# Expert rows gathered earlier: one-head selections first, scores after each query tile, eight seats from the start

## The chip, the cores and the metric

The kernel runs on one core of a Trainium2 chip. The metric is the device time of one execution in microseconds (us), the median of three runs. The engines are named as in the profile: PE (matrix products), DVE (vector work), ACT (activations and copies), POOL (elementwise work, and the issue of indirect transfers) and SP (the issue of plain transfers). A core has 16 DMA engines, which serve the queues of SP, ACT and POOL.

## The reference, cut to what matters

Two transformer blocks run over 256 tokens of width 1024. The change lies in the second half of the first block, a feed-forward layer that picks single-neuron experts by product keys:

```
def chunk(xc):                                   # 128 tokens
    q = (xc @ w_pq).reshape(P_CHUNK, P_HEADS, 2, P_DK // 2)
    s = jnp.einsum('thpd,hpkd->thpk', q, sub_keys)
    s_top, i_top = lax.top_k(s, P_TOPK)
    cand = s_top[..., 0, :, None] + s_top[..., 1, None, :]
    best, ci = lax.top_k(cand.reshape(P_CHUNK, P_HEADS, P_TOPK * P_TOPK), P_TOPK)
    ...
    expert = e1 * N_KEYS + e2
    gate = jax.nn.softmax(best.astype(jnp.float32), axis=-1).astype(xc.dtype)
    act = jax.nn.gelu(jnp.einsum('thkd,td->thk', u_tab[expert], xc), approximate=False)
    return jnp.einsum('thk,thkd->td', gate * act, v_tab[expert])
```

Each of the 256 tokens has 8 heads with 16 picks each. Each pick reads one row of `u` and one of `v`, 1024 floats each. The kernel keeps the two side by side in one table `uv`, so a pick is one row of 8 KB. Tokens lie on the 128 partitions in two tiles. One gather fetches one pick of all 128 tokens of a tile, 1 MB, so there are 2 x 8 x 16 = 256 gathers (`PICKED`), 268 MB together.

## The kernel before, in words

Every engine has one program, in a fixed order; waits on counters (semaphores) are all that ties the engines together. The work around the change, in order:

- **Query tiles.** PE makes eight tiles `pq0` to `pq7` of 512 columns, one head each (two key halves). `pq0` is a plain product. The fourteen halves of the others are split products: ACT rounds a block of the weights (`weight_round(c)`), POOL subtracts to get the rest (the loop over `SPLITS`, one step per c), and PE adds three products (L680 twice, then L685). `pq m` uses the blocks c = `AT_PQ` + 2m - 2 and + 2m - 1. I write "split +6" for the POOL step of c = `AT_PQ` + 6.
- **Scores.** After every second query tile, PE makes two score tiles (one for each token tile) of two heads. ACT copies query and score tiles out of PSUM (L1226 is the helper that records every activation).
- **Selection.** DVE takes `UNITS` one by one, in `select`. A unit is a token tile and two heads. It finds the 16 best of each key half (`top16`), the 16 best sums, and the rows' numbers, and then counts `index_ready` up. At some points in it, `keep_up` slips in dot products that are due (`dots_due`).
- **The picks.** For pick q: POOL issues the gather into seat q % 8 (`gather`, L1635). DVE makes the dot product of the u half with the token (`dot`, L1911). ACT makes a diagonal matrix from GELU of it times the gate (`weigh`). PE adds the v half, scaled by it, to the sum (`add_rows`, L853) and counts `v_done` up. Gather q waits for `v_done` of pick q - 8, whose seat it takes.
- **Seats.** The eight seats of 8 KB per partition lie one after the other in the arena from 16384. The last three overlap what the split products of the query tiles read (`h_hi`, `top_lo`, `top_hi2`). So five gathers are issued ahead of split +9, and the rest after `pq7`.
- **Weights.** SP fills three ring buffers in order (`load`), each when a counter `w_used` says that its last user is through. `keys` go between the first and the second block of `w_pq`. Near the end of the picks, five blocks of the next block's `w_in2` (2 MB each) are issued: two into the arena (`in2_early`), three into the ring. After the last pick, PE turns the sums over and the next block's products begin.

Of the kernel before, what the change touches and what calls it, by code (L numbers as in the profile page):

```python
# [24 lines left out]
ACT = mybir.ActivationFunctionType  # L25
# [26 lines left out]
UNITS = [(t, h, 2) for t in range(TT) for h in range(0, PH, 2)]  # L52
# [70 lines left out]
def dots_due(calls):  # L123


    return max(0, 3 * (calls - 4) // 2)
# [55 lines left out]

def tile_plan():
# [4 lines left out]
    def add(name, n, reader):  # L188
        first[name] = len(readers)
        readers.extend([reader] * n)  # L190
# [17 lines left out]
    for m in range(8):  # L208
        add(f"pq{m}", 1, "act")
        if m % 2:  # L210
            add(f"scores0_{m // 2}", 1, "act")
            add(f"scores1_{m // 2}", 1, "act")
        if m == 1:
            add("tokens0", 1, "dve")
# [28 lines left out]
def build(nc, w, out):  # L243
# [3 lines left out]
    with ExitStack() as ctx:  # L247
# [104 lines left out]
        keys = ar(12288, 16 * P)  # L352
# [7 lines left out]
        seats = [ar(16384 + 2 * D * i, 2 * D) for i in range(SEATS)]  # L360
# [145 lines left out]
        def _(sp):  # L506
# [24 lines left out]
            for i in range(4):  # L531
                load(STREAM["w_pq"] + i, w["w_pq"][i])
                if i == 0:
                    sp.wait_ge(conv_proj, 4)
                    sp.dma_start(keys, w["keys"]).then_inc(in_keys, 16)

            sp.wait_ge(dot_done, PICKED - 2)
            for i in range(2):
                sp.dma_start(in2_early[i], w["w_in2"][i]).then_inc(in2_loaded[i], 16)
            for i in range(9):  # L540
                load(STREAM["w_in2"] + i, w["w_in2"][2 + i])
# [46 lines left out]
        def _(pe):  # L588
# [269 lines left out]
            def scores(t, g, frees):  # L858

                ps = tile(TILE[f"scores{t}_{g}"])  # L860
                for j in range(4):
                    hp = 4 * g + j
                    last = group(ps[:, j * P:(j + 1) * P],
                                 [(qpT[:, hp, t * P:(t + 1) * P], keys[:, hp * P:(hp + 1) * P])], 0 if j else frees)
                last.then_inc(tile_ready, 1)

            for m in range(8):
                ps = tile(TILE[f"pq{m}"])
                for j in range(2):
                    frees = 1 if (2 * m + j) % 4 == 0 else 0  # L870
                    if m == 0:
                        last = plain(ps[:, j * T:(j + 1) * T], use(STREAM["w_pq"]), j, hT, None if j else h_part, 1, frees)
                    else:
                        c = AT_PQ + 2 * m - 2 + j
                        last = split(ps[:, j * T:(j + 1) * T], c, c + 1, h_hi, top_lo, frees,
                                     (h_split, K) if m + j == 1 else None)
                last.then_inc(tile_ready, 1)
                if m % 2:
                    if m == 1:
                        pe.wait_ge(in_keys, 16)  # L880
                    pe.wait_ge(tile_free["act"], readers[:TILE[f"pq{m}"] + 1].count("act"))
                    for t in range(TT):
                        scores(t, m // 2, 1 if m == 7 and t == 0 else 0)
                    if m == 1:
                        by_rows(0)
                if m >= 5:
                    for q in (2 * m - 10, 2 * m - 9):
                        add_rows(q)
            for q in range(6, PICKED - 1):
                if q == PICKED // TT - SEATS:  # L890
                    pe.wait_ge(gate_ready, len(UNITS))
                    by_rows(1)
                if q == PICKED // TT:
                    pe.wait_ge(dot_done, q)
                add_rows(q)
# [320 lines left out]
        def _(act):  # L1216
# [205 lines left out]
            for m in range(8):  # L1422
                if m:
                    for c in range(AT_PQ + 2 * m + 1, min(AT_PQ + 2 * m + 3, SPLITS)):
                        weight_round(c)
                ps = take(TILE[f"pq{m}"])
                fn(flat(qpT[:, 2 * m:2 * m + 2, :]), ps[:, :], ACT.Copy).then_inc(tile_free["act"], 1)
                if m % 2:
                    for t in range(TT):
                        ps = take(TILE[f"scores{t}_{m // 2}"])  # L1430
                        fn(sc[:, t, 2 * m - 2:2 * m + 2, :].rearrange("p a b -> p (a b)"), ps[:, :],
                           ACT.Copy).then_inc(tile_free["act"], 1)
                if m == 3:
                    gates_exp(0)
                if m >= 5:
                    for q in (2 * m - 10, 2 * m - 9):
                        weigh(q)
            for q in range(6, PICKED):
# [172 lines left out]
        def _(pool):  # L1611
# [26 lines left out]
            for c in range(SPLITS):  # L1638
                if c == AT_PQ + 9:
                    for q in range(5):  # L1640
                        gather(q)
# [17 lines left out]
            pool.wait_ge(tile_ready, TILE["pq7"] + 1)  # L1659
            for q in range(5, PICKED):  # L1660
                gather(q)
# [12 lines left out]
        def _(dve):  # L1674
# [239 lines left out]
            def select(u, between):  # L1914
# [4 lines left out]
                for i in range(2 * nh):  # L1919
                    hp = 2 * h0 + i  # L1920
                    if hp % 4 == 0:
                        score = TILE[f"scores{t}_{hp // 4}"]
                        dve.wait_ge(tile_free["act"], readers[:score + 1].count("act"))
# [560 lines left out]
```

## Time and profile before

| | |
|---|---|
| median of 3 runs | 1595.55 us (1595.25 to 1600.18) |
| the profiled execution's own time | 1595.38 us |
| its span | 1593.6 us |
| mean granted clock of PE | 0.979 |
| busy, share of the span | PE 88%, DVE 55%, ACT 36%, POOL 30% |
| gathers (queue q0) | 268.45 MB of 475.86 MB |

The span runs from the first to the last recorded instruction. Times below are microseconds from its start. Busy time alone tells little here, since the kernel is a row of stages with different limits. The stage of the change lies between about 380 and 1090.

### The profile page before, as it was taken

To read this page: it belongs to the slowest core of one execution; us is meant where nothing else is said; L and a number is where in the kernel's file an instruction comes from. 1 tells how busy PE (TensorE), PEld (TensorE's weight loads), DVE (VectorE), ACT (ScalarE), POOL (GpSimd) and SP (SyncE) were. 2 spreads that over 40 slices of the span, in tenths; PEclk is the share of its full clock that TensorE was granted. 3 is DMA by queue.
4 is the path that set the end of the run, shared out by engine and by line. 5 is a ranking of instruction groups with operands and counts; after the bars stand their busy time and mean duration, and the time that the engine had idled before them with its cause. 6 is when DMAs were issued, how large, how long until landed. Compare 5 with 4: busy or idle time off the path is not lost.

```text
span 1593.6 us, 17624 instructions
## 1 busy us (share of the span) xinstructions
PE 1402.7 (88%) x6500; PEld 845.1 (53%) x6500; DVE 871.5 (55%) x2048; ACT 578.8 (36%) x1078; POOL 478.4 (30%) x379
## 2 busy tenths in 40 slices
PE   6999999998878777878777777779999999899997
PEld 3888766697743232322222222226778987455544
DVE  2699675554659999844444444444437532412113
ACT  2244364433433433433333333335485411212112
POOL 0556400165533333333333333330435500000000
PEclk9999999999999999999999999999999999999999
DMA  9457521052379999999999999997133247799994
GB/s 384 189 233 292 211 93 67 25 214 103 135 299 422 421 421 421 421 421 422 421 421 422 422 421 421 421 411 298 53 141 124 107 167 310 280 427 428 428 427 199
DMA packets 53076, 475.86 MB, mean 299 GB/s; under 512 B 6144, under 2 KB 6784, under 8 KB 7552
## 3 DMA queue, kind: packets, MB, share of 16 engines
q0 software_dynamic: 36864, 268.45, 40.6%
q1 hardware_dynamic: 14832, 203.46, 31.8%
q10 hardware_dynamic: 1296, 2.84, 0.5%
q8 instruction: 51, 0.84, 0.2%
q14 instruction: 33, 0.27, 0.0%
HBM read 473.68 MB, written 1.05 MB: 298 GB/s over the span
## 4 chain that ended last, share of the span: by engine, by line
PE 52%; DMA 32%; DVE 10%; ACT 4%; issue 2%; POOL 1%; SPq 0%; DVEq 0%; ACTq 0%; POOLq 0%
DMA arena<-in_uv,pick 26%; PE psD L607 15%; PE psD L680 8%; PE psD L1103 6%; PE psY L853 5%; PE psD L685 4%; DVE arena L1911 4%; PE psD L1112 3%; ACT arena L1226 2%; DMA arena<-in_experts 2%; DMA ring<-in_w_mod 2%; PE psY L788 2%; DMA ring<-in_w_in 2%; PE psD L803 1%; PE psY L773 1%
## 5 line engine op out<-in xcount | busy, mean ns | idle before, releaser
L853 PE MATMUL psY<-arena 128*128 128x512 f32 x1024 | 513.4, 632 | 135.8 <-ACT arena L1226 133.9
L853 PEld LDWEIGHTS psY<-arena 128*128 128x128 f32 x1024 | 183.1, 196 | 462.6 <-ACT arena L1226 310.1
L1635 POOL DMA_INDIRECT arena<-in_uv,pick x256 | 240.7, 940 | 397.6 <-PE psY L853 372.8
L1226 ACT ACTIVATE arena<-cst,pick 128x128 f32<-128x128 f32 x256 | 102.9, 402 | 396.8 <-DVE pick L1911 393.8
L1911 DVE CUSTOM_DVE_ANT_0 arena<-arena,psD 128x1024 f32<-128x1024 f32 x128 | 156.3, 1221 | 162.5 <-DMA arena<-in_uv,pick 162.5
L1911 DVE CUSTOM_DVE_ANT_0 arena<-arena,psY 128x1024 f32<-128x1024 f32 x128 | 154.7, 1216 | 86.2 <-DMA arena<-in_uv,pick 85.6
L1226 ACT ACTIVATE arena<-psD 64x512 f32<-64x512 f32 (+4 forms) x128 | 68.3, 538 | 286.4 <-PE psD L1103 105.5
L1226 ACT ACTIVATE arena<-arena 128x128 f32<-128x128 f32 (+3 forms) x299 | 129.7, 434 | 17.1 <-DVE arena L2260 3.8
L1656 POOL TENSOR_TENSOR ring_r<-ring,work_r 128x1024 fp32r<-128x1024 f32 x19 | 46.5, 2460 | 159.1 <-ACT work_r L1226 159.0
L607 PE MATMUL psD<-arena 128*128 128x256 f32 (+4 forms) x352 | 90.3, 399 | 4.0 <-ACT arena L1226 2.4
L1752 DVE SCALAR_TENSOR_TENSOR psY<-arena,pick,psY 128x256 f32<-128x256 f32 x224 | 89.2, 482 | 0.0
L607 PE MATMUL psD<-arena,ring 128*128 128x256 f32 (+1 forms) x304 | 74.2, 402 | 4.0 <-issue 3.5
L1226 ACT ACT_TABLE_LOAD x56 | 71.8, 1283 | 7.4 <-DVE pick L1911 4.8
L607 PEld LDWEIGHTS psD<-arena 128*128 128x128 f32 (+2 forms) x352 | 60.1, 190 | 16.4 <-issue 3.5
L607 PEld LDWEIGHTS psD<-arena,ring 128*128 128x128 f32 x304 | 58.7, 195 | 15.8 <-issue 7.0
L2332 DVE TENSOR_TENSOR yrow_lo<-psD,yrow_hi 64x512 fp32r<-64x512 f32 x32 | 22.0, 689 | 71.4 <-ACT yrow_hi L1226 70.9
L685 PE MATMUL psD<-h_hi,ring_r 128*128 128x256 f32 x336 | 47.5, 284 | 1.0 <-POOL ring_r L1656 0.9
L1226 ACT ACTIVATE arena<-psY 128x512 f32<-128x512 f32 x47 | 27.9, 596 | 54.5 <-PE psY L773 35.9
L685 PEld LDWEIGHTS psD<-h_hi,ring_r 128*128 128x128 f32 x336 | 43.3, 192 | 1.8 <-POOL ring_r L1656 1.8
L1226 ACT ACTIVATE arena<-xh 128x512 f32<-128x512 f32 (+1 forms) x17 | 11.9, 705 | 76.1 <-DVE xh L2197 57.2
L2325 DVE SCALAR_TENSOR_TENSOR arena<-psD,arena 64x512 f32<-64x512 f32 x16 | 12.1, 756 | 48.0 <-ACT arena L1226 47.8
L1103 PE MATMUL psD<-arena,xh 128*64 128x512 f32 x160 | 36.5, 594 | 1.2 <-DMA arena<-in_experts 1.1
(381 smaller groups left out, 2390.2 us busy)
## 6 DMA issues: line engine op xcount, KB each, us to landing
arena<-in_experts SPq DMA_DIRECT2D x30, 2048.0 KB, 19.9
ring<-in_w_in SPq DMA_DIRECT2D x18, 2048.0 KB, 10.0
ring<-in_experts SPq DMA_DIRECT2D x18, 2048.0 KB, 18.2
ring<-in_w_mod SPq DMA_DIRECT2D x12, 2048.0 KB, 9.3
ring<-in_w_pq SPq DMA_DIRECT2D x4, 2048.0 KB, 7.9
ring<-in_w_out SPq DMA_DIRECT2D x3, 2048.0 KB, 8.1
ring<-in_w_pw SPq DMA_DIRECT2D x2, 2048.0 KB, 8.1
ring<-in_w_o SPq DMA_DIRECT2D x2, 2048.0 KB, 10.6
```

The source lines that it names most:

```text
L607: last = nc.tensor.matmul(dst, a, b, start=(i == 0), stop=(i == len(pairs) - 1))
L680: last = nc.tensor.matmul(ps, hi[:, k * P:(k + 1) * P], x[:, k, :], start=(k + i == 0), stop=False)
L685: last = nc.tensor.matmul(ps, lo[:, k * P:(k + 1) * P], x_hi[:, k, :], start=False, stop=(k == K - 1))
L788: last = nc.tensor.matmul(aux(m // 2 % 2)[:, (m % 2) * T:(m % 2 + 1) * T], wt[:, k * 512 + (m % 4) * P:k * 512 + (m % 4 + 1) * P], convz[: ...
L853: last = nc.tensor.matmul(y_of[t][:, h * 512:(h + 1) * 512], diag[:, q % DIAGS, :], seats[q % SEATS][:, D + h * 512:D + (h + 1) * 512], st ...
L1103: last = nc.tensor.matmul(psD[bank][lo:lo + 64, :], lhs, wt[:, col:col + 512], start=(k == 0), stop=(k == K - 1))
L1112: last = nc.tensor.matmul(psD[bank][lo:lo + 64, :], hidT[:, f, 64 * side:64 * (side + 1)], wd[:, f * D + 8 * lo:f * D + 8 * lo + 512], sta ...
L1226: return nc.scalar.activation(dst, src, f, **kw)
L1635: nc.gpsimd.indirect_dma_start(seats[q % SEATS], None, w["uv"], bass.IndirectOffsetOnAxis(index[:, q:q + 1], 0)).then_inc(gathered[q % SEA ...
L1656: nc.gpsimd.tensor_tensor(split_at(ring_r, c), split_at(ring, c), split_hi(c).bitcast(F32), ALU.subtract).then_inc(u_lo_ready, 1)
L1752: s[j % 2] = mark(stt(cpart if j == TAPS - 2 else acc, y[:, j:j + T], conv_w[:, m * TAPS + j:m * TAPS + j + 1], acc, ALU.mult, ALU.add))
L1911: nc.vector.tensor_tensor_reduce(u_row, u_row, rows_of[t], 1.0, 0.0, ALU.mult, ALU.add, dots[:, q:q + 1]).then_inc(dot_done, 1)
```

## The change

1. The first unit of two heads becomes two units of one head, so there are nine.
2. Score tiles hold one head for both token tiles, and follow each query tile (`pick_order`): `pq0`, tokens, scores 0, `pq1`, then `pq m`, scores m - 1, and scores 7 last.
3. The eight seats move: one to 10432, five stay at 16384, and two go into the ring buffer of the second `w_pq` block. `keys` move to 12480, into space that holds `merged` until `x_ready` reaches 8, so their load waits for that.
4. Gathers 0 to 5 are issued ahead of split +6, gathers 6 and 7 ahead of +8 (after `pq3`), 8 and 9 ahead of +10, 10 to 14 ahead of +12, and the rest after +13.
5. Sums 0 and 1 follow scores 3, sums 2 to 6 scores 4, 7 to 11 scores 5, and 12 to 17 scores 6 (`ADDS`).
6. `keep_up` counts from the first call, not the fourth.
7. SP issues the two early blocks of `w_in2` and two ring blocks when `v_done` is 249. Before, all five went when `dot_done` was 254. The fifth, whose buffer holds the last two seats, now waits for `v_done` 256.

```diff
-UNITS = [(t, h, 2) for t in range(TT) for h in range(0, PH, 2)]
+UNITS = [(0, 0, 1), (0, 1, 1)] + [(t, h, 2) for t in range(TT) for h in range(0, PH, 2) if t or h]
+ADDS = [0, 0, 0, 0, 2, 7, 12, 18]
...
-    return max(0, 3 * (calls - 4) // 2)
+    return max(0, 3 * (calls - 1) // 2)
...
+def pick_order():
...
+    order = [("pq", 0), ("tokens", 0), ("scores", 0), ("pq", 1)]
+    for m in range(2, PH):
+        order += [("pq", m), ("scores", m - 1)]
+    return order + [("scores", PH - 1)]
...
-        keys = ar(12288, 16 * P)
+        keys = ar(12480, 16 * P)
...
-        seats = [ar(16384 + 2 * D * i, 2 * D) for i in range(SEATS)]
+        pq1 = ring[(STREAM["w_pq"] + 1) % RING]
+        seats = ([ar(10432, 2 * D)] + [ar(16384 + 2 * D * i, 2 * D) for i in range(5)] +
+                 [pq1[:, 0:2 * D], pq1[:, 2 * D:4 * D]])
...
                 if i == 0:
-                    sp.wait_ge(conv_proj, 4)
+                    sp.wait_ge(x_ready, K)
                     sp.dma_start(keys, w["keys"]).then_inc(in_keys, 16)
 
-            sp.wait_ge(dot_done, PICKED - 2)
+            sp.wait_ge(v_done, PICKED - SEATS + 1)
             for i in range(2):
                 sp.dma_start(in2_early[i], w["w_in2"][i]).then_inc(in2_loaded[i], 16)
-            for i in range(9):
+            for i in (1, 2, 0, 3, 4, 5, 6, 7, 8):
+                if i == 0:
+                    sp.wait_ge(v_done, PICKED)
                 load(STREAM["w_in2"] + i, w["w_in2"][2 + i])
...
+            for kind, m in pick_order():
+                if kind == "pq":
+                    pq(m)
+                elif kind == "tokens":
+                    by_rows(m)
+                else:
+                    scores(m)
+                    if 2 <= m < PH - 1:
+                        for q in range(ADDS[m], ADDS[m + 1]):
+                            add_rows(q)
+            for q in range(ADDS[-1], PICKED - 1):
...
+                    if m == 1:
+                        gates_exp(0)
+                    if 2 <= m < PH - 1:
+                        for q in range(ADDS[m], ADDS[m + 1]):
+                            weigh(q)
...
             for c in range(SPLITS):
-                if c == AT_PQ + 9:
-                    for q in range(5):
+                if c == AT_PQ + 6:
+                    for q in range(6):
+                        gather(q)
+                if c == AT_PQ + 8:
+                    pool.wait_ge(tile_ready, TILE["pq3"] + 1)
+                    for q in range(6, SEATS):
+                        gather(q)
+                if c == AT_PQ + 10:
+                    for q in range(SEATS, SEATS + 2):
+                        gather(q)
+                if c == AT_PQ + 12:
+                    for q in range(SEATS + 2, SEATS + 7):
                         gather(q)
...
-            pool.wait_ge(tile_ready, TILE["pq7"] + 1)
-            for q in range(5, PICKED):
+            for q in range(SEATS + 7, PICKED):
                 gather(q)
```

POOL's program around the query tiles, before (`ring_r<-ring` is a split, `in_uv,pick` a gather):

```order
57 L1656 TENSOR_TENSOR ring_r<-ring,top_hi 128x1024 [waits u_hi_ready]
58 L1635 DMA arena<-in_uv,pick 128x2048 [waits index_ready]
59 L1635 DMA arena<-in_uv,pick 128x2048 x4
60 L1656 TENSOR_TENSOR ring_r<-ring,work_r 128x1024 [waits u_hi_ready] x2
61 L1656 TENSOR_TENSOR ring_r<-ring,top_hi 128x1024 [waits u_hi_ready]
62 L1656 TENSOR_TENSOR ring_r<-ring,work_r 128x1024 [waits u_hi_ready] x2
63 L1635 DMA arena<-in_uv,pick 128x2048 [waits tile_ready]
64 L1635 DMA arena<-in_uv,pick 128x2048 x2
65 L1635 DMA arena<-in_uv,pick 128x2048 [waits v_done] x24
```

The row ahead of the five gathers is split +8. The five splits behind them are +9 to +13. After the change, from split +5 on:

```order
55 L1681 TENSOR_TENSOR ring_r<-ring,top_hi 128x1024 [waits u_hi_ready]
56 L1650 DMA arena<-in_uv,pick 128x2048 [waits index_ready]
57 L1650 DMA arena<-in_uv,pick 128x2048 x5
58 L1681 TENSOR_TENSOR ring_r<-ring,work_r 128x1024 [waits u_hi_ready] x2
59 L1650 DMA ring<-in_uv,pick 128x2048 [waits tile_ready]
60 L1650 DMA ring<-in_uv,pick 128x2048
61 L1681 TENSOR_TENSOR ring_r<-ring,top_hi 128x1024 [waits u_hi_ready]
62 L1681 TENSOR_TENSOR ring_r<-ring,work_r 128x1024 [waits u_hi_ready]
63 L1650 DMA arena<-in_uv,pick 128x2048 [waits v_done] x2
64 L1681 TENSOR_TENSOR ring_r<-ring,work_r 128x1024 [waits u_hi_ready]
65 L1681 TENSOR_TENSOR ring_r<-ring,top_hi 128x1024 [waits u_hi_ready]
66 L1650 DMA arena<-in_uv,pick 128x2048 [waits v_done] x4
```

Fifteen gathers now stand among the splits, and seven of these wait for sums. SP's program at the end of the picks, before (`in_w_in` of L539 are the two early blocks, of L512 the ring's):

```order
30 L512 DMA ring<-in_w_pq 128x4096 [waits w_used] x3
31 L539 DMA arena<-in_w_in 128x4096 [waits dot_done]
32 L539 DMA arena<-in_w_in 128x4096
33 L512 DMA ring<-in_w_in 128x4096 [waits w_used] x9
34 L512 DMA ring<-in_w_bsb 128x4096 [waits w_used]
```

The same place after the change:

```order
30 L520 DMA ring<-in_w_pq 128x4096 [waits w_used] x3
31 L547 DMA arena<-in_w_in 128x4096 [waits v_done]
32 L547 DMA arena<-in_w_in 128x4096
33 L520 DMA ring<-in_w_in 128x4096 [waits w_used] x2
34 L520 DMA ring<-in_w_in 128x4096 [waits w_used,v_done]
35 L520 DMA ring<-in_w_in 128x4096 [waits w_used] x6
```

Four blocks now stand ahead of the wait for the last sum, and all four may be issued while gathers are still under way.

## Rows read from the trace of the kernel before

**Rows 1.** The page: GB/s in 40 slices; the gathers' queue.

```profile
GB/s 384 189 233 292 211 93 67 25 214 103 135 299 422 421 421 421 421 421 422 421 421 422 422 421 421 421 411 298 53 141 124 107 167 310 280 427 428 428 427 199
...
q0 software_dynamic: 36864, 268.45, 40.6%
```

**Rows 2.** Windows: busy us of PE, PEld, DVE, ACT, POOL; clock, DMA share, GB/s.

```profile
422.00:424.00 2.00, 0.42 (x1) 0.43 (x2) 1.93 (x10) 1.86 (x5) 0.79 (x1) 0.72 0.09 37
424.00:426.00 2.00, 2.00 (x3) 0.75 (x3) 1.93 (x4) 0.25 (x1) 0.00 (x0) 0.50 0.05 12
...
428.00:447.00 19.00, 17.49 (x108) 13.90 (x106) 0.00 (x0) 3.10 (x7) 2.40 (x1) 0.96 0.00 0
```

**Rows 3.** POOL in order of time: start, duration, what, idle before and its releaser.

```profile
400.80 2.40 POOL L1656 TENSOR_TENSOR ring_r<-ring,work_r 128x1024 fp32r<-128x1024 f32 x1 [0.48 <-ACT work_r L1226]
...
407.26 1.15 POOL L1635 DMA_INDIRECT arena<-in_uv,pick  x1 [1.22 <-DVE pick L1988]
...
412.45 0.94 POOL L1635 DMA_INDIRECT arena<-in_uv,pick  x1 [0.30 <-issue]
...
447.18 0.95 POOL L1635 DMA_INDIRECT arena<-in_uv,pick  x1 [11.21 <-PE psD L685]
...
495.22 0.94 POOL L1635 DMA_INDIRECT arena<-in_uv,pick  x1 [5.06 <-PE psY L853]
...
1065.95 0.94 POOL L1635 DMA_INDIRECT arena<-in_uv,pick  x1 [1.54 <-PE psY L853]
```

**Rows 4.** DVE in order of time: selection, the first late dot, the last dot.

```profile
390.67 0.30 DVE L1886 MAX8 arena<-arena 128x8 f32<-128x128 f32 x1 [13.63 <-ACT arena L1226]
...
406.78 0.19 DVE L1988 TENSOR_TENSOR pick<-psD,arena 128x32 uint32<-128x32 f32 x1
...
452.62 1.22 DVE L1911 CUSTOM_DVE_ANT_0 arena<-arena,psY 128x1024 f32<-128x1024 f32 x1 [25.85 <-DMA arena<-in_uv,pick]
...
1081.30 1.22 DVE L1911 CUSTOM_DVE_ANT_0 arena<-arena,psD 128x1024 f32<-128x1024 f32 x1 [1.24 <-DMA arena<-in_uv,pick]
```

**Rows 5.** PE in order of time: last of pq0, two score tiles, sums.

```profile
376.83 5.39 PE L812 MATMUL psD<-xh,ring 128*128 128x256 f32 x20 [0.19 <-DVE xh L1877]
...
418.63 2.05 PE L607 MATMUL psD<-arena 128*128 128x128 f32 x16 [0.86 <-ACT arena L1226]
423.57 6.73 PE L853 MATMUL psY<-arena 128*128 128x512 f32 x8 [2.90 <-ACT arena L1226]
...
437.45 3.70 PE L853 MATMUL psY<-arena 128*128 128x512 f32 x8 [1.41 <-ACT arena L1226]
```

**Rows 6.** The chain in order of time: one half of a query tile.

```profile
409.13 1.92 PE psD L680 x16
411.05 0.96 PE psD L685 x8
```

**Rows 7.** ACT in order of time: copy of a score tile, then a table load.

```profile
420.71 0.60 ACT L1226 ACTIVATE arena<-psD 128x512 f32<-128x512 f32 x1 [0.29 <-PE psD L607]
421.33 1.28 ACT L1226 ACT_TABLE_LOAD   x1
```

**Rows 8.** SP at the end of the picks, in order of time.

```profile
1077.61 0.80 SPq L539 DMA_DIRECT2D arena<-in_w_in  x2
```

**Rows 9.** PE at the end of the picks, in order of time.

```profile
1066.18 1.98 PE L853 MATMUL psY<-arena 128*128 128x512 f32 x4 [0.50 <-ACT arena L1226]
...
1083.73 1.88 PE L853 MATMUL psY<-arena 128*128 128x512 f32 x4
...
1088.22 8.42 PE L607 MATMUL psD<-arena 128*128 128x256 f32 x32 [0.74 <-DVE arena L2024]
```

**Rows 10.** DMA queues in 1096 to 1098: packets, MB, share of 16 engines.

```profile
q1 hardware_dynamic: 44, 0.69, 80.3%
q10 hardware_dynamic: 45, 0.16, 19.7%
```

**Rows 11.** The same in 1079 to 1080: the gathers' queue.

```profile
q0 software_dynamic: 3, 0.02, 5.8%
```

More of the change, by code:

```diff
@@ L207, in tile_plan @@
     add("out", 4, "dve")
[L208 to L214, printed above, removed]
+    for kind, n in pick_order():
+        add(f"{kind}{n}", 1, "dve" if kind == "tokens" else "act")
     add("tokens1", 1, "dve")
@@ L856, in add_rows, with pq @@
                 last.then_inc(v_done, 1)
[L858 to L867, printed above, removed]
+            def pq(m):
                 ps = tile(TILE[f"pq{m}"])
@@ L877, in _, with scores @@
                 last.then_inc(tile_ready, 1)
[L878 to L889, printed above, removed]
+            def scores(m):
+                if m == 0:
+                    pe.wait_ge(in_keys, 16)
+                pe.wait_ge(tile_free["act"], readers[:TILE[f"pq{m}"] + 1].count("act"))
+                ps = tile(TILE[f"scores{m}"])
+                for t in range(TT):
+                    for j in range(2):
+                        hp, at = 2 * m + j, (2 * t + j) * P
+                        last = group(ps[:, at:at + P], [(qpT[:, hp, t * P:(t + 1) * P], keys[:, hp * P:(hp + 1) * P])],
+                                     1 if m == PH - 1 and t + j == 0 else 0)
+                last.then_inc(tile_ready, 1)
+            for kind, m in pick_order():
[9 more added lines that the diff above has]
+            for q in range(ADDS[-1], PICKED - 1):
                 if q == PICKED // TT - SEATS:
@@ L1420, in weigh @@
                 fn(d, d, ACT.Copy, scale=gate[:, q:q + 1]).then_inc(diag_ready, 1)
[L1422 to L1438, printed above, removed]
+            for kind, m in pick_order():
+                if kind == "pq":
+                    if m:
+                        for c in range(AT_PQ + 2 * m + 1, min(AT_PQ + 2 * m + 3, SPLITS)):
+                            weight_round(c)
+                    ps = take(TILE[f"pq{m}"])
+                    fn(flat(qpT[:, 2 * m:2 * m + 2, :]), ps[:, :], ACT.Copy).then_inc(tile_free["act"], 1)
+                elif kind == "scores":
+                    ps = take(TILE[f"scores{m}"])
+                    fn(sc[:, :, 2 * m:2 * m + 2, :].rearrange("p t a b -> p t (a b)"),
+                       ps.rearrange("p (t n) -> p t n", t=TT), ACT.Copy).then_inc(tile_free["act"], 1)
+                    if m == 1:
[3 more added lines that the diff above has]
+                            weigh(q)
+            for q in range(ADDS[-1], PICKED):
                 weigh(q)
@@ L1920, in select @@
                     hp = 2 * h0 + i
-                    if hp % 4 == 0:
-                        score = TILE[f"scores{t}_{hp // 4}"]
-                        dve.wait_ge(tile_free["act"], readers[:score + 1].count("act"))
+                    if hp % 2 == 0:
+                        dve.wait_ge(tile_free["act"], readers[:TILE[f"scores{hp // 2}"] + 1].count("act"))
                     top16(sc[:, t, hp, :], sc2[:, i, :], sv[:, i, :], si[:, i, :])
```

## The prediction, made before the changed kernel ran

> **What bounds the kernel now.** I read the page first. From slice 13 on its GB/s row stands at 421 or 422 and hardly moves until the picks are over, and the gathers' queue carries 268.45 MB in 36864 packets, 144 for each gather [rows 1]. So in this stage the DMA engines set the time: one gather is 1.0486 MB, and 1.0486 / 421 gives **2.49 us**. DVE, ACT and PE follow it. The windows then show where DMA is not full. Five gathers run early, are through by 422, and DMA carries nothing from 428 to 447 [rows 2]. POOL's timeline says why: gather 4 goes out at 412.45, gather 5 at 447.18, released by the last query tile on PE [rows 3]. DVE meanwhile stands 25.85 us before dot 5 [rows 4]. Two things follow. First, whatever fills that hole, or starts gather 0 sooner, takes its length off the end of the picks, if DMA then stays full. Second, the last dot (1081.30) is followed at once by sums and the next block, with PE waiting for DVE and not for a load at 1088.22 [rows 4, 9]. What delays the last gather delays the whole kernel.
>
> **The start of the gathers.** pq0 ends at 376.83 + 5.39 = 382.2 [rows 5]. The tokens' transposes lie beside ACT's copy of pq0, so scores 0 can run from 383.0. Two score tiles take 2.05 [rows 5], one 1.0, its copy 0.6 [rows 7]: selection begins at 384.7, where it began at 390.67. The first unit took 406.97 - 390.67 = 16.3 us to its row numbers [rows 4]. With one head the searches halve and the small operations don't, so it lies between 8 and 16 us. I take 10, since the searches are most of it: 394.8. POOL must have done splits up to +5, one in 2.4 us [rows 3], and is free at about 395.3. Gather 0 goes out at **395.5**, not 407.26. The six take 1.15 + 5 x 1.25 = 7.4 us of POOL [rows 3], so split +6 ends at 405.3. PE reaches its use of it at 405.3 too, so that costs nothing; were the unit 3 us slower, PE would stand 3 us.
>
> `keys` now wait for `x_ready`, and the second `w_pq` block queues behind them on SP: 3 MB, 7.5 us at 421. The residual is complete before the norm and pq0 [rows 5] come, and `keys` and the block are wanted only behind these. I put this at nothing; if the cover were short, everything behind pq0 would be late by what is missing, and I see no more than 3 us of that.
>
> **The pace from there.** From idle DMA, gather 5 was issued at 447.18 and dotted at 452.62, so a gather lands 5.4 us after its issue, or 2.49 after the one before it. Gathers 8 and up need the sum eight picks before. Now PE sets that: half a query tile takes 1.92 + 0.96 = 2.88 [rows 6], a tile 5.8, a score tile 1.0, a sum 3.70 / 2 = 1.85 [rows 5]. My schedule, in the order of the new program:
> pq1 384.0 to 389.8; pq2, scores 1 to 396.6; pq3, scores 2 to 403.4; pq4, scores 3 to 410.2. Then PE stands 2.9 us for ACT's copy, a table load of 1.28 and two activations, as it did at 423.57 [rows 5, 7]. There the granted clock fell to 0.50 and two sums took 6.73 instead of 3.70 [rows 2, 5]. I expect the same here: sums 0 and 1 end at 416.5 and 419.8. pq5 and scores 4 to 426.6, 1.5 of waiting, sums 2 to 6 (with 0.6 for the tables of the second unit's exponent) to 438.2. pq6 and scores 5 to 445.0, sums 7 to 11 from 446.6 to 455.9. pq7 and scores 6 to 462.7, sums 12 to 17 from 464.3 to 475.4, scores 7 to 476.4. Then ACT loads tables twice more, and sum 18 ends at 482.8.
>
> Landings by that: gathers 0 to 7 from 400.9 to 418.3 without a hole; 8 and 9 at 422.0 and 425.4; 10 (issued 430.1) at 435.5 and 14 at 445.5; 15 (448.6) at 454.0, 19 at 464.0; 20 (466.3) at 471.7, 25 at 484.1; 26 (482.8) at 488.2. So the holes are not gone but cut into five, 20 us together: with eight seats and sums at set places, PE recycles only 2, 5, 5 and 6 of them between query tiles. From gather 26 on seats come back at 1.85 each, faster than 2.49, and DMA stays full as it did before. In the kernel before gather 26 was issued later than its data needed (495.22, rows 3), with a backlog: it landed at 452.6 + 21 x 2.49 = 504.9. The gain is **504.9 - 488.2 = 16.7**. One DMA engine trails the others: the last landing is 1081.30, not 452.6 + 250 x 2.49 = 1075.1, and at 1079 the gathers' queue still moves three packets a microsecond [rows 11]. Holes let it catch up, so I add 1.8, a third of that lag: **-18.5**. Bounds: -10 if the sums come 7 us later than drawn, -38 if no hole remains (11.8 earlier start and 27 of hole).
>
> **The end of the gathers.** This is where I look for the price. Four blocks of `w_in2`, 8.4 MB, now go out when `v_done` is 249. Sum 248 ran at 1066.18 for 1.98 [rows 9], so in the old frame that is 1068.2, against 1077.61 before [rows 8], when only the last gather and a half was on the way. Counted from 1069, with the last landing at 1081.30, 12.3 us of gathers are left, 4.9 of them. How do two queues share? Where SP's and ACT's queues both had work, each moved as many packets as the other, 44 and 45, and the bytes went by packet size, 80.3% to 19.7% [rows 10]. A gather's row is 8 KB, a block's row 16 KB. One for one, gathers get a third of the bandwidth, and the last lands when all four blocks are through: 8.4 / 421 = 19.9 us late. The last gather before kept its 2.49 although blocks had begun [rows 11, 4], so what an engine already holds isn't pushed back; that is worth about one packet in nine: **+19**. Bounds: 0 if gathers go first; 20 if all four go between.
>
> The Trainium skill ("DMA: Bandwidth & Descriptors", "Queues, rings and completion order") says that an engine goes round the queues by whole packets of some 9 to 17 descriptors. By that a gather and a block would alternate, and four blocks would pass ahead of the last gather, 20 us. The rows above don't agree with so coarse a turn, since ACT's small transfer moved evenly beside SP's, yet the price is nearly the same.
>
> With a gather every 7.5 us PE stands long enough for the lower clock, and the last sum (1.88, rows 9) and the turns beside it slow down as the two sums at 423.57 did, 6.73 - 3.70 = **+3** (0 to 7). Nothing comes back for the blocks' earlier arrival, since PE did not wait for them at 1088.22 [rows 9]. The fifth block waits for the last sum, but is wanted only behind the products that start at 1088.22, and takes 5 us: nothing.
>
> **Other edits.** The number of query, score and add instructions stays. One more unit costs DVE some 3 us of small operations, hidden while it waits for gathers. Its second unit waits for ACT's exponent until about 430, behind scores 4; dots 7 to 11 are due by 446 and done by 442.
>
> **Sum.** 1595.4 - 18.5 + 19 + 3 = 1598.9; the profiled time of 1595.38 and the median of 1595.55 are the same for this purpose. I say 1598.5. What a measurement of this kernel tells from no change is about 0.3%, 4.8 us.
>
> **The rivals.**
> (a) What I expect, gain and loss nearly equal: 0.42, of which 0.36 within 0.3% and 0.06 above.
> (b) Gathers are not held up by blocks of another queue. For it: the last gather's even pace; against it: the equal packet counts [rows 10]. Then only the start counts, 1577 to 1580. 0.27.
> (c) The start gains more, because ACT or the clock let the sums come sooner and the holes shrink: each microsecond at sum 18 is one at the end. Holes of 10 instead of 20 give 1588.5. Nothing in the rows shortens PE's own 95 us from 382 on except the clock's 3. 0.13.
> (d) Slower: the DVE queue decides. Its second unit is behind an exponent that ACT does only after scores 4; if dots 7 to 11 are late, PE stands with pq6 done and pq7 behind the sums, and every later gather moves. From 5 us of it the end is slower than before by over 0.3%: 1604, at 8 us 1607. For it is that DVE has only 4 us to spare by my schedule; against it, that its dots are done in time by the same schedule. 0.18.
> That the change doesn't do what it says I give nothing: the order above shows it.
>
> **Range and chances.** The likeliest case alone gives 1593 to 1604. The range takes in (b) and most of (d): 1577 to 1605. Faster by over 0.3% is (b) and (c), 0.40; within 0.3% 0.36; slower is (d) and the top of (a), 0.24.
>
> **What would show it.** First gather at 395 (393 to 401); GB/s not zero between 428 and 447 but with holes near 427, 447 and 465; sums of 3.3 us for the first two; gather 26 issued near 483. At the end, the time from the issue of the first `w_in2` block to the last dot: 13 us if gathers go first, 32 if they share. It is this number on which the prediction stands or falls; the second is the issue of gather 26.

## The result and the profile after

The changed kernel takes **1601.24 us** (median of 8 runs, 1598.42 to 1604.7) where the kernel before takes 1595.4 beside it (8 runs, 1590.66 to 1600.18). The ratio is 1.0038, interval 1.0023 to 1.0053: 5.8 us slower. I had said 1598.5 and 1577 to 1605. The profiled execution has a span of 1596.4 us, against 1593.6 before.

The page of the changed kernel: GB/s in 40 slices, and the gathers' queue.

```profile
GB/s 392 198 221 309 186 106 53 54 106 222 310 324 392 421 421 421 420 421 421 422 421 422 421 422 421 421 401 86 53 135 130 107 161 316 272 428 428 427 427 203
...
q0 software_dynamic: 36864, 268.45, 40.8%
```

Beside [rows 1] the middle is the same 421. Slices 10 to 12 carry more (222, 310, 324 for 103, 135, 299), and slice 13 a little less. Bytes and packets of the gathers are the same. So the change acts at the two ends of the picks. First the start. POOL in order of time, first the one-head unit's gathers, then those that wait for a sum behind each query tile:

```profile
392.98 1.15 POOL L1650 DMA_INDIRECT arena<-in_uv,pick  x1 [0.17 <-issue]
...
405.28 0.96 POOL L1650 DMA_INDIRECT ring<-in_uv,pick  x1 [0.16 <-issue]
...
414.77 0.96 POOL L1650 DMA_INDIRECT arena<-in_uv,pick  x1 [2.60 <-PE psY L863]
...
427.67 0.96 POOL L1650 DMA_INDIRECT arena<-in_uv,pick  x1 [4.30 <-PE psY L863]
...
445.54 0.96 POOL L1650 DMA_INDIRECT ring<-in_uv,pick  x1 [4.30 <-PE psY L863]
...
462.44 0.94 POOL L1650 DMA_INDIRECT arena<-in_uv,pick  x1 [9.10 <-PE psY L863]
...
480.07 0.94 POOL L1650 DMA_INDIRECT arena<-in_uv,pick  x1 [8.11 <-PE psY L863]
```

These are gathers 0, 6, 8, 10, 15, 20 and 26. Gather 0 goes out 14.3 us sooner than in [rows 3] and gather 26 15.2 sooner. Part of that isn't the change's: pq0 ends at 374.19 + 5.32 = 379.5, 2.7 us sooner than in [rows 5]. Over the changed kernel and the variants of it that follow it ends anywhere from 379.5 to 383.8, though up to there they are all the same program. I count from the end of pq0 from here on. The windows (busy us of PE, PEld, DVE, ACT, POOL; clock, DMA share, GB/s) show four holes where [rows 2] has one. The last row is the whole stretch with them: 317 of 421 GB/s over 91 us is 22 us of DMA time not used.

```profile
422.00:428.00 6.00, 4.59 (x24) 3.06 (x23) 0.32 (x2) 5.39 (x10) 1.70 (x2) 1.00 0.07 26
...
443.00:446.00 3.00, 2.72 (x7) 1.29 (x8) 1.90 (x5) 2.87 (x9) 0.46 (x1) 1.00 0.16 68
...
460.00:463.00 3.00, 2.81 (x7) 1.38 (x8) 2.66 (x9) 2.81 (x9) 0.56 (x1) 1.00 0.13 55
...
480.00:482.00 2.00, 2.00 (x4) 0.80 (x3) 1.97 (x8) 1.53 (x4) 0.94 (x1) 0.62 0.45 98
...
483.00:600.00 117.00, 95.82 (x199) 37.19 (x197) 105.62 (x353) 45.80 (x103) 46.74 (x51) 0.96 1.01 419
...
399.00:490.00 91.00, 78.76 (x345) 50.15 (x344) 65.24 (x210) 39.14 (x78) 43.97 (x36) 0.92 0.82 317
```

Then the end. SP in order of time: the four `w_in2` blocks, two from each row.

```profile
1049.53 0.80 SPq L547 DMA_DIRECT2D arena<-in_w_in  x2
1050.38 0.91 SPq L520 DMA_DIRECT2D ring<-in_w_in  x2
```

DVE, the last five dots:

```profile
1052.74 1.22 DVE L1935 CUSTOM_DVE_ANT_0 arena<-arena,psD 128x1024 f32<-128x1024 f32 x1 [1.25 <-DMA arena<-in_uv,pick]
1058.91 1.22 DVE L1935 CUSTOM_DVE_ANT_0 arena<-arena,psD 128x1024 f32<-128x1024 f32 x1 [4.94 <-DMA arena<-in_uv,pick]
...
1066.28 1.22 DVE L1935 CUSTOM_DVE_ANT_0 arena<-arena,psD 128x1024 f32<-128x1024 f32 x1 [6.14 <-DMA arena<-in_uv,pick]
...
1073.67 1.22 DVE L1935 CUSTOM_DVE_ANT_0 ring<-ring,psD 128x1024 f32<-128x1024 f32 x1 [6.16 <-DMA ring<-in_uv,pick]
...
1081.00 1.22 DVE L1935 CUSTOM_DVE_ANT_0 ring<-ring,psD 128x1024 f32<-128x1024 f32 x1 [6.10 <-DMA ring<-in_uv,pick]
```

From the moment the blocks are out the dots come first 6.2 and then 7.4 us apart, not 2.5. The chain of the same stretch says what the end waits for, a gather that takes 33.70 us to land:

```profile
1047.28 33.70 DMA ring<-in_uv,pick
...
1081.00 1.22 DVE ring L1935
```

The two DMA queues in 1055 to 1060, then in 1070 to 1075 (packets, MB, share of 16 engines):

```profile
q1 hardware_dynamic: 104, 1.61, 75.5%
q0 software_dynamic: 76, 0.52, 24.7%
...
q1 hardware_dynamic: 130, 1.88, 88.6%
q0 software_dynamic: 7, 0.04, 2.0%
```

PE at the same end, against the 1.98, 1.88 and 8.42 of [rows 9]: a late sum at the lower clock, the last sum, and the next block.

```profile
1075.88 3.44 PE L863 MATMUL psY<-ring,arena 128*128 128x512 f32 x4 [3.67 <-ACT arena L1241]
...
1084.04 2.70 PE L863 MATMUL psY<-ring,arena 128*128 128x512 f32 x4
...
1089.36 8.42 PE L617 MATMUL psD<-arena 128*128 128x256 f32 x32 [0.73 <-DVE arena L2047]
```

### The profile page after: what moved, and what is told of

The parts are those of the page before. It is cut to its first block, busy times and chain, and to the rows that moved or that the text cites. A ratio compares the mean times of both kernels' runs of the same rounds, so it can differ in the third digit from the quotient of the medians.

```text
span 1596.4 us, 17667 instructions
## 1 busy us (share of the span) xinstructions
PE 1403.1 (88%) x6500; PEld 848.7 (53%) x6500; DVE 875.0 (55%) x2076; ACT 579.4 (36%) x1081; POOL 478.8 (30%) x379
## 4 chain that ended last, share of the span: by engine, by line
PE 54%; DMA 29%; DVE 9%; ACT 4%; issue 2%; POOL 1%; SPq 0%; DVEq 0%; ACTq 0%; POOLq 0%
DMA ring<-in_uv,pick 21%; PE psD L617 15%; PE psD L690 8%; PE psY L863 8%; PE psD L1118 6%; PE psD L695 4%; PE psD L1127 3%; DMA arena<-in_uv,pick 3%; ACT arena L1241 2%; DMA arena<-in_experts 2%; DVE ring L1935 2%; PE psY L798 2%; DMA ring<-in_w_in 2%; DVE arena L1935 1%; ACT L1241 1%
## 5 line engine op out<-in xcount | busy, mean ns | idle before, releaser
L863 PE MATMUL psY<-arena 128*128 128x512 f32 x768 | 389.9, 640 | 111.5 <-ACT arena L1241 111.2
L863 PEld LDWEIGHTS psY<-arena 128*128 128x128 f32 x768 | 139.8, 198 | 355.1 <-ACT arena L1241 237.4
L1650 POOL DMA_INDIRECT arena<-in_uv,pick x192 | 180.6, 940 | 309.0 <-PE psY L863 300.7
L1935 DVE CUSTOM_DVE_ANT_0 arena<-arena,psD 128x1024 f32<-128x1024 f32 x96 | 117.2, 1221 | 131.1 <-DMA arena<-in_uv,pick 131.1
L863 PE MATMUL psY<-ring,arena 128*128 128x512 f32 x256 | 126.7, 622 | 27.4 <-ACT arena L1241 27.3
L1935 DVE CUSTOM_DVE_ANT_0 arena<-arena,psY 128x1024 f32<-128x1024 f32 x96 | 115.9, 1215 | 41.6 <-DMA arena<-in_uv,pick 41.1
L1241 ACT ACTIVATE arena<-arena 128x128 f32<-128x128 f32 (+2 forms) x300 | 129.7, 433 | 17.1 <-DVE arena L2283 3.8
L863 PEld LDWEIGHTS psY<-ring,arena 128*128 128x128 f32 x256 | 45.9, 194 | 106.6 <-ACT arena L1241 67.9
L1650 POOL DMA_INDIRECT ring<-in_uv,pick x64 | 60.1, 940 | 86.7 <-PE psY L863 86.2
L1935 DVE CUSTOM_DVE_ANT_0 ring<-ring,psD 128x1024 f32<-128x1024 f32 x32 | 39.1, 1221 | 50.0 <-DMA ring<-in_uv,pick 50.0
```

The costliest lines, as they stand in the source:

```text
L863: last = nc.tensor.matmul(y_of[t][:, h * 512:(h + 1) * 512], diag[:, q % DIAGS, :], seats[q % SEATS][:, D + h * 512:D + (h + 1) * 512], st ...
L1241: return nc.scalar.activation(dst, src, f, **kw)
L1650: nc.gpsimd.indirect_dma_start(seats[q % SEATS], None, w["uv"], bass.IndirectOffsetOnAxis(index[:, q:q + 1], 0)).then_inc(gathered[q % SEA ...
L1935: nc.vector.tensor_tensor_reduce(u_row, u_row, rows_of[t], 1.0, 0.0, ALU.mult, ALU.add, dots[:, q:q + 1]).then_inc(dot_done, 1)
```

## The experiments

My theory: the start gains about 16 to 18 us, and the blocks beside the last gathers take it all back. The first rival: the start gains little and the blocks cost little. Nine kernels follow, each timed beside the kernel before, whose median was then 1595.4 to 1596.6. The table holds what the traces show, one profiled execution of each kernel, as distances, so that the spread of the stage ahead of pq0 drops out: from the end of pq0 to the start of gather 0, from there to the start of the last dot, from there to the next block's first product, and on to the end of the span.

```
kernel             median   ratio [interval]           pq0-g0  g0-dot  dot-block  block-end
before             1595.4   1                           25.0   674.0     6.9      505.4
changed            1601.2   1.0038 [1.0023, 1.0053]     13.5   688.0     8.4      507.0
late4              1578.9   0.9895 [0.9880, 0.9910]     13.5   669.6     6.9      507.8
before_early       1612.6   1.0103 [1.0088, 1.0119]     25.0   692.0     9.1      505.0
two_early          1590.7   0.9968 [0.9957, 0.9979]     13.5   682.0     6.8      504.9
quarter_pieces     1583.5   0.9920 [0.9904, 0.9937]     13.5   673.8     6.8      507.2
late4_after_dots   1583.9   0.9924 [0.9904, 0.9945]     13.5   669.5     9.1      507.7
late4_two_heads    1600.7   1.0031 [1.0018, 1.0044]     28.4   674.3     6.9      507.2
late4_keep         1578.1   0.9894 [0.9878, 0.9909]     13.5   666.5     6.9      506.8
late4_sums         1576.8   0.9884 [0.9869, 0.9899]     13.5   665.4     6.9      508.2
late4_sums_keep    1573.5   0.9857 [0.9838, 0.9876]     13.5   662.5     6.9      508.2
```

**late4.** The blocks wait for the dots again, everything else stays.

```diff
             sp.wait_ge(v_done, PICKED - SEATS + 1)
+            sp.wait_ge(dot_done, PICKED - 2)
```

> The changed kernel, with the four w_in2 blocks waiting for dot 254 as before, besides v_done 249. Theory 1 (the gain at the start was there, and blocks that share DMA with the last gathers took it back): the last gathers keep their 2.48 us, and the time is 20 to 25 us below the changed kernel, 1576 to 1581, and 15 to 19 below the kernel before. Rival (the gathers' DMA time is fixed and the new start brings little): within 4 us of the changed kernel, 1597 to 1605.

Measured 1578.85. SP, the last dot and the next block in its trace:

```profile
1059.10 0.80 SPq L548 DMA_DIRECT2D arena<-in_w_in  x2
```

```profile
1060.24 1.22 DVE L1936 CUSTOM_DVE_ANT_0 ring<-ring,psD 128x1024 f32<-128x1024 f32 x1 [1.23 <-DMA ring<-in_uv,pick]
...
1062.72 1.22 DVE L1936 CUSTOM_DVE_ANT_0 ring<-ring,psD 128x1024 f32<-128x1024 f32 x1 [1.24 <-DMA ring<-in_uv,pick]
```

The last gathers come 2.48 us apart to the end, and one line gives back 22.4 us by the medians. The two traces differ by 19.0 only; the profiled execution of the changed kernel was its fastest of eight, 1598.42 against the median of 1601.24. From pq0 to the last dot it is 683.1 us, against 699.1 before and 701.5 in the changed kernel: the start gains 16.0, the blocks cost 18.4.

**before_early.** The kernel before, with the changed kernel's early blocks alone.

```diff
-            sp.wait_ge(dot_done, PICKED - 2)
+            sp.wait_ge(v_done, PICKED - SEATS + 1)
```

> The kernel before, with one edit: the w_in2 blocks are issued at v_done 249 instead of dot 254. All five blocks go out here, since no seat lies in the ring. Theory 1: the last four gathers land 7.4 us apart instead of 2.48, and the time is 20 to 25 us above before, 1615 to 1621. Rival (the tail costs only together with the new seats, or not at all): 1593 to 1599.

Measured 1612.63, 17.2 us slower and 2.4 below the expected range. DVE's last dots:

```profile
1092.04 1.22 DVE L1911 CUSTOM_DVE_ANT_0 arena<-arena,psD 128x1024 f32<-128x1024 f32 x1 [6.15 <-DMA arena<-in_uv,pick]
...
1099.40 1.22 DVE L1911 CUSTOM_DVE_ANT_0 arena<-arena,psD 128x1024 f32<-128x1024 f32 x1 [6.13 <-DMA arena<-in_uv,pick]
```

The same 7.4 us, and the last dot 18.0 us later from gather 0. The cost is that of the blocks' moment, whatever the start does. It is also not that of their number: five blocks were out by 1070.14 here, and cost what four cost in the changed kernel. One block's worth passes ahead of each gather that is left, and there are four such gathers in both.

**two_early.** The changed kernel with two early blocks, the ring's two held until dot 254.

```diff
                 sp.dma_start(in2_early[i], w["w_in2"][i]).then_inc(in2_loaded[i], 16)
+            sp.wait_ge(dot_done, PICKED - 2)
```

> The changed kernel, with the two early blocks at v_done 249 and the two ring blocks at dot 254. If DMA packets alternate one for one, half the bytes cost half: two of the four late gathers are 7.4 us apart, and the time lies 10 to 11 us below the changed kernel, near 1590. If the loss came from the mere start of loads beside gathers, or from the lower PE clock, it would stay near 1600; if it came only from the ring blocks (whose buffers lie beside the last two seats), near 1579.

Measured 1590.65: 10.6 us of the 22.4 are back with half the bytes. The trace is less even. Up to the last dot only 6.0 of the 18.4 are back (682.0 beside 688.0 and 669.6). DVE's last dots:

```profile
1068.71 1.22 DVE L1936 CUSTOM_DVE_ANT_0 arena<-arena,psD 128x1024 f32<-128x1024 f32 x1 [6.12 <-DMA arena<-in_uv,pick]
...
1072.39 1.22 DVE L1936 CUSTOM_DVE_ANT_0 ring<-ring,psD 128x1024 f32<-128x1024 f32 x1 [2.45 <-DMA ring<-in_uv,pick]
...
1077.32 1.22 DVE L1936 CUSTOM_DVE_ANT_0 ring<-ring,psD 128x1024 f32<-128x1024 f32 x1 [3.70 <-DMA ring<-in_uv,pick]
```

Two gathers are 6.2 and 7.4 us apart, as expected; the last is 4.9, because the two ring blocks that went out at 1069.97 still met it.

**quarter_pieces.** The same four blocks at the same moment, in pieces of 4 KB a partition, with the waits on them raised to match.

```diff
-                sp.dma_start(in2_early[i], w["w_in2"][i]).then_inc(in2_loaded[i], 16)
+                for c in range(0, SLOT, 1024):
+                    sp.dma_start(in2_early[i][:, c:c + 1024], w["w_in2"][i][:, c:c + 1024]).then_inc(in2_loaded[i], 16)
...
-                sp.dma_start(ring[idx % RING][:, 0:n], src).then_inc(w_loaded[idx % RING], 16)
+                for c in (range(0, n, 1024) if idx in PIECES else (0,)):
+                    e = c + 1024 if idx in PIECES else n
+                    sp.dma_start(ring[idx % RING][:, c:e], src[:, c:e]).then_inc(w_loaded[idx % RING], 16)
```

> The changed kernel, with the four w_in2 blocks that start at the 249th sum each loaded as four loads of 4 KB a partition instead of one of 16 KB; same bytes, same moment, same queue. Theory (the engines take one packet of each queue in turn, whatever its size; the gathers' packets are 8 KB and the blocks' 16 KB, so the gathers get a third): with 4 KB packets the gathers get two thirds, the last ones come some 3.7 us apart instead of 7.4, the last dot is 8 to 12 us sooner after the first block's issue than the 31.5 us of the changed kernel, and the kernel takes 1588 to 1594 us. Rival 1 (the engines share by bytes, or the whole of one queue's ring entries goes first): the last gathers stay 7.4 us apart and the time within 2 us of the changed kernel's 1601. Rival 2 (sixteen starts on SP instead of four cost more than they give): slower than the changed kernel.

Measured 1583.54, 17.7 us faster than the changed kernel and 4 beyond the expected range. DVE's last dots, then the queues in 1061 to 1065:

```profile
1057.55 1.22 DVE L1943 CUSTOM_DVE_ANT_0 arena<-arena,psD 128x1024 f32<-128x1024 f32 x1 [2.22 <-DMA arena<-in_uv,pick]
...
1065.14 1.22 DVE L1943 CUSTOM_DVE_ANT_0 ring<-ring,psD 128x1024 f32<-128x1024 f32 x1 [2.54 <-DMA ring<-in_uv,pick]
...
1068.89 1.22 DVE L1943 CUSTOM_DVE_ANT_0 ring<-ring,psD 128x1024 f32<-128x1024 f32 x1 [2.53 <-DMA ring<-in_uv,pick]
```

```profile
q1 hardware_dynamic: 424, 1.54, 96.3%
q0 software_dynamic: 14, 0.10, 5.9%
```

Three gaps in 11.34 us are 3.78 each, as expected; I had only multiplied wrongly, for four gaps of 3.6 us less are 14.4, and the last dot came 14.2 sooner. The sum for one DMA engine: a gather is 1.0486 / 16 = 65.5 kB on it, eight rows of 8 KB, and takes 2.49 us alone. At that rate 7.37 us carry 194 kB, so 128 kB of a block pass per gather, eight packets of 16 KB; 3.78 us carry 99.5 kB, so 34 kB pass, eight packets of 4 KB. **Sharing goes by packets, not by bytes**: rival 1 of this run falls. Eight for eight would also come of turns of eight, and the changed kernel's last microseconds tell the two apart. By then the other engines are through with the gathers, and what sets the last dots is one engine that trails, as in [rows 11]. The queues in 1077 to 1078 of the changed kernel, then the gathers' queue in 1066 to 1067 of this run:

```profile
q1 hardware_dynamic: 3, 0.05, 11.5%
q0 software_dynamic: 1, 0.01, 1.9%
...
q0 software_dynamic: 3, 0.02, 5.8%
```

The second row, one gather packet in one microsecond, is the same in each of the four from 1076 to 1080. Turns of eight would show three of them a microsecond, as in [rows 11], and then none for 4.9 us. The shares give the times: 1.9% of 16 us is 0.31 for a gather's packet, 11.5% is 0.61 for each block packet. One of each takes 0.92 us, and eight pairs 7.4, the distance of the dots. With the small pieces two, three and two gather packets pass in the three microseconds from 1065. So the engine takes **one packet of each queue in turn**.

**late4_after_dots.** The blocks wait for dot 256 instead of 254.

```diff
-            sp.wait_ge(dot_done, PICKED - 2)
+            sp.wait_ge(dot_done, PICKED)
```

> late4 with the wait ahead of the w_in2 loads moved from the 254th dot to the 256th, so that no load shares the engines with a gather at all, and the loads go out about 5 us later. Theory 1 (the last gathers are held up only by what runs beside them, and in late4 nothing does any more): the dots are where they are in late4, and the loads come 5 us late for the next block, which costs 0 to 5 us: 1579 to 1584. Theory 2 (late4 still loses to the overlap at its end): a gain of 1 to 3 us against late4.

Measured 1583.9. The dots don't move (669.5 and 669.6), and PE now waits for the load at the next block:

```profile
1074.21 8.86 PE L618 MATMUL psD<-arena 128*128 128x256 f32 x32 [2.87 <-DMA arena<-in_w_in]
```

Theory 1: 254 costs the gathers nothing, and two dots later costs the next block 2 us in the trace and 5 by the medians. Of these two moments the old one is the better.

**late4_two_heads.** Every unit holds two heads again, and `keep_up` counts from the fourth call; score tiles, seats and the places of the gathers stay changed.

```diff
-UNITS = [(0, 0, 1), (0, 1, 1)] + [(t, h, 2) for t in range(TT) for h in range(0, PH, 2) if t or h]
+UNITS = [(t, h, 2) for t in range(TT) for h in range(0, PH, 2)]
...
-    return max(0, 3 * (calls - 1) // 2)
+    return max(0, 3 * (calls - 4) // 2)
```

> late4 with every top-k unit of two heads as before, so that gather 0 waits for the selection of two heads (12.5 us later by the changed kernel's own rows); everything else of the change stays. Theory (the one-head units carry most of what the change gives at the start): the row of gathers starts 12 us later and ends about 12 us later, 1589 to 1593 us, near the time of the kernel before. Rival (the start is paced by the sums between query tiles, not by when the first gather goes out): at most 4 us slower than late4, 1579 to 1583.

Measured 1600.67, 21.8 us above late4 and 8 beyond what I expected. I had reckoned 12.5 us for gather 0; the trace has 28.4 - 13.5 = 14.9, and then 4.7 more up to the last dot. DVE's selection shows the first part:

```profile
386.35 0.29 DVE L1911 MAX8 arena<-arena 128x8 f32<-128x128 f32 x1 [7.59 <-ACT arena L1242]
...
398.75 0.29 DVE L1911 MAX8 arena<-arena 128x8 f32<-128x128 f32 x1 [9.16 <-ACT arena L1242]
```

The second head's scores now come one query tile later, so a two-head unit stands 9.16 us for them. Cut scores without cut units are **worse** than the kernel before: gather 0 comes 3.4 us later from pq0 than there. Together the two edits bring gather 0 11.5 us sooner from pq0 (25.0 and 13.5), most of the 16.0 gained. One-head units with the old score tiles weren't run, and how much of the 4.7 is due to `keep_up` isn't shown.

**late4_keep.** Filler matmuls on PE between score tile 3 and sum 0, so that the clock doesn't fall while PE stands for ACT.

```diff
                     scores(m)
+                    if m == 3:
+                        keep(3, aux(2))
```

> As late4, and three idle 128x512 products on PE between scores 3 and sum 0, so that PE doesn't stand 2.9 us there. They write the half of PSUM that sum 0 begins anew. If the granted clock fell because PE stood, sums 0 and 1 take 3.7 us instead of 6.7, everything up to sum 18 is 3 us earlier, and the time is 2 to 3 us below late4. If the clock falls for another reason, the time is that of late4 or up to 1 us above it.

Measured 1578.08, 0.8 us below late4, where 2 to 3 were expected; that small a difference is within the error. The trace shows more. The filler takes 2.74 us, and sum 0 begins 31.2 us behind pq0 with it and without it, so it delays nothing. The granted clock at the sums is 1.00 instead of 0.50, and sums 0 and 1 take 3.70 instead of 6.67. Gather 26 goes out 3.0 us sooner from pq0, and the last dot comes 3.1 sooner from gather 0.

**late4_sums.** More sums at each stop between query tiles.

```diff
-ADDS = [0, 0, 0, 0, 2, 7, 12, 18]
+ADDS = [0, 0, 0, 0, 2, 8, 17, 28]
...
-                    for q in range(SEATS, SEATS + 2):
+                    for q in range(SEATS, SEATS + ADDS[4]):
...
-                    for q in range(SEATS + 2, SEATS + 7):
+                    for q in range(SEATS + ADDS[4], SEATS + ADDS[5]):
...
-            for q in range(SEATS + 7, PICKED):
+            for q in range(SEATS + ADDS[5], PICKED):
```

> late4 with the hand table of sums moved forward: sums 2 to 7 after score tile 4, 8 to 16 after score tile 5, 17 to 27 after score tile 6 (late4: 2 to 6, 7 to 11, 12 to 17), with the gathers ahead of the later splits moved to match. Theory (the start is paced by when sums free seats, which shows as three stretches of 3 us with q0 nearly empty in the changed kernel, near 425, 444 and 461): more sums per stop fill the last two of them, so gather 26 goes out some 5 us sooner than in late4 and the kernel takes about 1573 us (1571 to 1576). Rival 1 (the DVE, which does the dots between pieces of its selection, is the pace): the dots come no sooner, TensorE stands at the sums instead, and the time stays within 1.5 us of late4. Rival 2 (TensorE's query tiles are pushed back and the selection with them): slower than late4 by 2 to 5 us.

Measured 1576.78, 0.8 us above the expected range. In the trace gather 26 goes out 5.4 us sooner from pq0 than in late4, as expected, and the last dot comes 4.2 sooner from gather 0. The medians, from two different comparisons, give 2.1, so the size rests on one trace of each. Part of it is the clock: in late4 PE stands 4.38 us ahead of its first sums behind score tile 7 and does four of them in 9.86 us. First late4, then late4_sums, PE at that place:

```profile
476.19 9.86 PE L864 MATMUL psY<-arena 128*128 128x512 f32 x16 [4.38 <-ACT arena L1242]
```

```profile
476.75 7.13 PE L864 MATMUL psY<-arena 128*128 128x512 f32 x16 [1.71 <-ACT arena L1242]
```

**late4_sums_keep.** Both.

> late4 with both small additions, the sums moved forward in the hand table and the filler matmuls ahead of sum 0: if the two gains measured apart (1.7 and 0.8 us by the medians, each near what its measurement can tell) add up, 1576 us (1574.5 to 1578), the fastest of all. If the filler only delays sum 0 as it shortens it, and the sums' table already covers that, it is 1576 to 1578, as with the table alone.

Measured **1573.46**, the fastest, and 1 us below the expected range: 23 us under the kernel before and 28 under the changed one. From gather 0 to the last dot it is 7.1 us less than late4, 3.1 and 4.2 added; the medians give 5.4, 3.3 of it from late4_sums to here, for the filler.

## Why the prediction was right, and where it wasn't

- **What bounds the kernel**: right. DMA at 421, both ends of the picks decide, and the chain's 33.70 us gather says so again.
- **First gather at 395.5**: pq0-g0 was 13.5 us against 13.3 by my working. The one-head unit's row numbers were there at 391.99, 9.95 us behind its start at 382.04, where I took 10. As in my working it was split +5 that held the gather, here for the last 0.8 us. No engine stood for `keys`. DVE, then POOL:

```profile
391.82 0.17 DVE L2011 TENSOR_TENSOR pick<-psD,arena 128x16 uint32<-128x16 f32 x1
...
390.41 2.40 POOL L1681 TENSOR_TENSOR ring_r<-ring,top_hi 128x1024 fp32r<-128x1024 f32 x1 [0.46 <-ACT top_hi L1241]
```

- **The schedule by hand**: gather 26 was to go out 482.8 - 382.2 = 100.6 us behind pq0, and went out at 480.07 - 379.5 = 100.6. Gathers 10, 15 and 20 are within 1.2 us of it too. The clock fell to 0.50 for sums 0 and 1, which took 6.65. The exact hit at gather 26 is in part luck: PE was through with scores 7 at 471.64, 2.1 us sooner from pq0 than drawn, and lost that again in sum 18, which took some 4 us at a granted clock of 0.50 where I had 1.85. The holes, drawn as 20 us, were 22.
- **The gain of 18.5**: it was 16.0. The 16.7 worked out from landings held. The 1.8 that I added because a trailing engine would catch up in the holes did not come. In late4, counted as I counted before, gather 26 lands at 480.25 + 5.4 = 485.7 and the last should at 485.7 + 229 x 2.49 = 1055.9. It came at 1062.72, a lag of 6.8 us and no smaller than the 6.2 before. The size of that term was a guess, and the holes did nothing of the kind.
- **The blocks, +19**: 18.4 by late4, 18.0 by before_early. Packet for packet, as [rows 10] had it. What I had wrong is why four blocks cost four blocks' time: not because all must be through first, but because four gathers were left, each behind eight block packets; a fifth block added nothing. My number to stand or fall by, from the first block's issue to the last dot, was 32 if they share; it was 1081.00 - 1049.53 = 31.5. Rival (b), 13 us, is out.
- **The skill's rule**: the Trainium skill ("DMA: Bandwidth & Descriptors", "Queues, rings and completion order") has an engine change queues only after a whole packet of many descriptors. The trace doesn't agree with a turn of that size: on the engine that trails one gather packet passes in each microsecond from 1076 to 1080, between block packets, so a turn is one row's packet. My price was the same by either, since eight for eight comes of both.
- **The lower clock, +3**: it came, but for 1.5 us: the last dot to the next block took 8.4 instead of 6.9. Late sums at the lower clock (3.44) lie in the wait for the next gather and cost nothing; on the path are only the turning over of the other sums (eight products in 1.97, before 1.04) and the last sum, which at 2.70 was part slow. The granted clock there was 0.57 and 0.58, before 1.00.
- **What I had at nothing and was not**: behind the next block's start the changed kernel takes 507.0 us, before 505.4. Over the eleven kernels this part lies between 504.9 and 508.2 and goes with no single edit; the cause stays open.
- **The sum**: -16.0 + 18.4 + 1.5 + 1.6 = +5.5, against +3.5 forecast, and the medians say +5.8. The profiled spans differ by 2.8 only, since pq0 came 2.7 us sooner in that execution. That the total came within 3 us is in part luck, for the 2.5 too much at the start and the 1.6 that I left out were offset by the 1.5 and 0.6 too much at the end. I had 0.24 on slower by over 0.3%, mostly for rival (d); it came out 0.38% slower by (a).
- **Rival (d)**: DVE did stand for ACT's exponent, as the row shows, until 427.64. That is 48.1 us behind pq0, and my 430 was 47.8, so it was no sooner than drawn.

```profile
427.64 0.17 DVE L1923 TENSOR_REDUCE gate_sum<-arena 128x1 f32<-128x16 f32 x1 [7.68 <-ACT arena L1241]
```

The dots it held back were done by 439, ahead of the sums that want them from 443 on, about the 4 us to spare that I had. Rival (c) didn't happen by itself, but late4_sums and late4_keep show it was there to be had.

## What to carry to other kernels

A load started "for free" beside the last transfers of a stage isn't free where DMA is the bound: it delays the last small one by its own packets, and where an engine takes one packet of each queue in turn, the queue with the large packets gets most of the bandwidth. Look at what waits for the last transfer, and start the next stage's loads when that one is nearly in; here starting them 9.6 us later was worth 22 us, and pieces a quarter as large, started as early, 18. And a change of several parts that comes out at nothing may hold one that is worth keeping: undo them one at a time, from both ends.

## What the hardware showed that I had not expected

One small DVE operation took 3.58 us at 408.62, where the same line took 0.18 for the unit before, at 387.49. DVE, then POOL at the same time in the changed kernel:

```profile
408.62 3.58 DVE L1973 TENSOR_TENSOR arena<-arena 128x16 f32<-128x16 f32 x1
```

```profile
407.51 2.36 POOL L1681 TENSOR_TENSOR ring_r<-ring,top_hi 128x1024 fp32r<-128x1024 f32 x1
409.82 2.35 POOL L1681 TENSOR_TENSOR ring_r<-ring,work_r 128x1024 fp32r<-128x1024 f32 x1
```

It ends when POOL's two splits end (412.17). This is not chance: in all eight kernels with one-head units the operation takes between 2.86 and 3.58 us, by when it begins beside the splits, and ends 0.02 to 0.05 us behind the second of them. In late4_two_heads, where no split runs beside it, the same line takes 0.19. Operations that read one input from PSUM keep their time beside a split (0.43 at 388.48). That POOL holds it up is argued from this; no run took the splits away with all else in place.
